# Gated linear attention behind its levels: state additions ahead, score products ahead of state products, two heads in turn, heads staggered

## Chip, cores and metric

The kernel runs on one core of one Trainium2 chip. The metric is the device time of one execution in microseconds (us); less is better. The time before is 3137.09 us, the median of three runs.

## What is computed

Two transformer blocks of two layers each. The change lies in the first layer of the second block, in its gated linear attention (GLA): 4 heads, keys of 64, values of 128, over 256 context tokens and 512 latent tokens, once forwards and once backwards in time. Cut to what matters:

```python
def gla_scan(q, k, v, loga, s0):              # chunk by chunk; loga: log of the decay of each key channel
    def step(S, inp):
        b = jnp.cumsum(ac, axis=2)
        ...
        attn = jnp.einsum('bhid,bhjd,bhijd->bhij', qc, kc, decay)
        o = attn @ vc + jnp.einsum('bhid,bhde->bhie', qc * jnp.exp(b), S)
        b_last = b[:, :, -1:, :]
        S_new = (jnp.exp(b_last[:, :, 0, :, None]) * S
                 + jnp.einsum('bhjd,bhje->bhde', kc * jnp.exp(b_last - b), vc))
...
    o_f, s_f = gla_scan(q, k, v, loga[0], s_f)
    o_b, s_b = gla_scan(flip(q), flip(k), flip(v), flip(loga[1]), s_b)
    o = o_f + flip(o_b)
    o = o * lax.rsqrt(jnp.mean(o * o, axis=-1, keepdims=True) + EPS)
    o = o.transpose(0, 2, 1, 3).reshape(B_, L, GLA_VAL_WIDTH) * g_gla.astype(jnp.float32)
    o = (o * jax.nn.silu(r.astype(jnp.float32))).astype(h.dtype)
    y = jnp.concatenate([fourier_mix(u_f), o], axis=-1) @ w_out
```

Each head's output is divided by its root mean square, scaled, multiplied by a gate and goes with the Fourier half into the output product `w_out`.

## The kernel before

Every engine has its own program in a fixed order, and semaphores join them: `k.tick(name, key)` counts up behind an instruction, `k.seen(name, key)` is what another engine (or the same) waits for. Nothing is reordered by a scheduler, so an instruction that waits holds up all that stands behind it on its engine. The data lie with features on partitions and tokens along the free dimension. There are 6 chunks of 128 tokens (`NC2`), and `f` counts two pairs of heads: heads 0 and 1 share one pair tile (head 0 on partitions 0 to 63, head 1 on 64 to 127), heads 2 and 3 the other.

The GLA stage has these parts.

- **Levels.** The scores with their decay are built in 14 steps (7 levels, forwards and backwards). In each, VectorE (DVE) makes an argument (L621, L622), ScalarE (ACT) takes its exponential (L628), DVE multiplies keys and queries in (L637), TensorE (PE) multiplies (L721), and DVE merges the result under a mask into `gatt` (L747). PE takes the heads there by turns, one on partitions 0 to 63, the next on 64 to 127 (`GL_UNITS`). The change doesn't touch the levels.
- **Decayed keys.** Behind the last merge DVE makes the argument for the forward keys (L2007), ACT the exponential (L1940), DVE the product with the keys (L2010). PE turns the result round by 12 transposes (L1892), ACT copies them out of PSUM (L1946), and the same `gcomb` is then used for the backward keys (L1948, L2010, L1892, L1946). Behind that come the decayed queries `e0` and `e1` (`gb` in the rows: L1949, L2012, L2013, L1951, L2015).
- **States.** For each of 5 steps and both directions PE makes the addition to the state, 4 matmuls (L1904, one per head, alternately into partitions 0 to 63 and 64 to 127 of PSUM), and DVE makes state = decay * state + addition (L2025, two instructions). In step n, PE waits for the backward state n. GpSimd (POOL) zeroes the first states (L1812) behind `e1`. The states lie over the queries and keys, in `z`.
- **Heads.** For each head and chunk PE adds up three products in PSUM: values with scores (L1918, contracted over 128 partitions), forward state with `e0` (L1919, over 64) and backward state with `e1` (L1920, over 64). Behind its 6 chunks the head is finished: ACT copies it out (L1957) and squares it (L1963), PE sums the squares over the partitions (L1924), ACT takes the root by Ln and Exp (L1968, L1971), DVE scales and gates (L2031, L2033), ACT and DVE split it into a high and a low part (L501, L507) for the output product. PE's next head follows its sum.
- **Output product.** `pe_out2` (L302 in the rows) waits for the low part of the last head.

The lines that order all this on PE and ACT:

```python
    for n in range(NC2 - 1):
        for d in range(2):
            ...
            if n:
                pe.wait_ge(*k.seen("state", ("g", 1, n)))
...
    for h in range(4):
        ...
        if h >= 2:
            pe.wait_ge(*k.seen("h_lo", ("gla", 4 + h - 2)))
...
            pe.wait_ge(*k.seen("squared", ("g", h, i)))
```

## Time and profile before

| | us |
|---|---|
| runs (three) | 3133.9, 3137.09, 3142.81 |
| median | 3137.09 |
| the profiled execution | 3133.24 |
| its span | 3131.9 |
| PE busy | 2682.8 (86%) |
| DVE busy | 1763.4 (56%) |
| ACT busy | 1063.2 (34%) |
| PE's share of the chain that ended last | 77% |
| the stage of the change, from the last merge to the output product | 1653.55 to 1748.59 |

The span runs from the first to the last instruction; the execution's own time has 1.3 us more around it. "Busy" is the time in which an engine ran instructions, and an engine that is busy need not be what the end waits for: that is told by the chain, followed back from the last instruction. PEclk is the clock that TensorE was granted, 1.0 for 2.4 GHz and 0.5 for 1.2 GHz. An fp32 matmul shows as two instructions, so "x48" on such a line are 24 matmuls; a transpose is one.

### The profile page before, as it was taken

The numbers are of one execution on the slowest core, as the hardware profiler recorded it, in microseconds if no ns is written. First come the engines' busy times: TensorE is split into PE (matmuls) and PEld (weight loads), VectorE is DVE, ScalarE is ACT, GpSimd is POOL, SyncE is SP. The second block draws the span as 40 slices with busy tenths as digits, with TensorE's granted clock in tenths as the row PEclk, the third lists the DMA queues.
The fourth block names the chain that finished last, engine by engine and source line by source line (L and its number), as shares of the span: only waits on it lengthen the run. The fifth ranks groups of instructions, "written<-read, shape, count | busy, mean of one in ns | idle before, by whom it ended". The sixth has DMA issues, their size and how long they took to land.

```text
span 3131.9 us, 31365 instructions
## 1 busy us (share of the span) xinstructions
PE 2682.8 (86%) x12792; PEld 2169.5 (69%) x12792; DVE 1763.4 (56%) x2386; ACT 1063.2 (34%) x1371; POOL 33.9 (1%) x52
## 2 busy tenths in 40 slices
PE   5956579999569999897676889999998866889998
PEld 4845458888448888685365778888886633578886
DVE  6574568888778877510483255424534155365464
ACT  3242253233343244422232253313324422254242
POOL 0000000000100000000200000000000000000000
PEclk9966789999779999999756899999998999999999
DMA  8700028855125666121000111211221100123232
GB/s 309 231 18 2 33 79 267 270 185 183 38 77 188 200 198 199 48 67 64 14 1 1 41 51 64 74 55 61 67 69 58 51 1 0 42 85 102 89 106 83
DMA packets 80270, 294.99 MB, mean 94 GB/s; under 512 B 8944, under 2 KB 11632, under 8 KB 79872
## 3 DMA queue, kind: packets, MB, share of 16 engines
q1 hardware_dynamic: 80128, 292.99, 28.6%
q8 instruction: 101, 1.65, 0.2%
q14 instruction: 41, 0.34, 0.0%
HBM read 290.86 MB, written 2.10 MB: 94 GB/s over the span
## 4 chain that ended last, share of the span: by engine, by line
PE 77%; DVE 13%; ACT 6%; issue 2%; DMA 0%; POOL 0%; SPq 0%; DVEq 0%; ACTq 0%
PE ps L302 65%; PE ps L721 2%; PE ps L2116 2%; PE ps L325 2%; PE ps L1744 1%; DVE anm L2243 1%; ACT h_hi L501 1%; DVE gatt L747 1%; ACT ascores L2195 1%; DVE h_lo L507 1%; ACT sq L1596 1%; DVE w_lo L283 1%; DVE aprobs L2218 1%; DVE x L1320 0%; DVE x L1333 0%
## 5 line engine op out<-in xcount | busy, mean ns | idle before, releaser
L302 PE MATMUL ps<-h_hi,w_hi 128*128 128x512 f32 (+1 forms) x2464 | 819.0, 369 | 68.5 <-DVE w_lo L283 38.4
L302 PE MATMUL ps<-h_hi,w_lo 128*128 128x512 f32 (+1 forms) x2464 | 815.8, 368 | 0.0
L302 PE MATMUL ps<-h_lo,w_hi 128*128 128x512 f32 (+1 forms) x2464 | 814.7, 367 | 0.0
L283 DVE TENSOR_TENSOR w_lo<-w_raw,w_hi 128x1024 fp32r<-128x1024 f32 (+2 forms) x323 | 414.7, 1284 | 617.4 <-ACT w_hi L275 616.6
L275 ACT ACTIVATE w_hi<-w_raw 128x1024 fp32r<-128x1024 f32 (+2 forms) x323 | 357.4, 1107 | 940.0 <-PE ps L302 917.5
L302 PEld LDWEIGHTS ps<-h_hi,w_hi 128*128 128x128 f32 x2464 | 466.1, 189 | 155.1 <-DVE w_lo L283 41.9
L302 PEld LDWEIGHTS ps<-h_lo,w_hi 128*128 128x128 f32 x2464 | 466.4, 189 | 77.4 <-issue 0.7
L302 PEld LDWEIGHTS ps<-h_hi,w_lo 128*128 128x128 f32 x2464 | 465.9, 189 | 77.6
L302 PE MATMUL ps<-g_hi,w_hi 128*128 128x512 f32 (+1 forms) x880 | 295.7, 369 | 0.8 <-DVE w_lo L283 0.8
L302 PE MATMUL ps<-g_lo,w_hi 128*128 128x512 f32 (+1 forms) x880 | 294.9, 368 | 0.0
L302 PE MATMUL ps<-g_hi,w_lo 128*128 128x512 f32 (+1 forms) x880 | 294.8, 368 | 0.0
L421 DVE CUSTOM_DVE_ANT_0 m_raw<-m_raw,c_act,small 128x1024 f32<-128x1024 f32 x179 | 226.4, 1280 | 2.8 <-DMA m_raw<-in_ada_w 2.8
L346 DVE SCALAR_TENSOR_TENSOR x<-ps,mods,x 128x512 f32<-128x512 f32 (+1 forms) x112 | 75.3, 690 | 211.7 <-PE ps L302 211.6
L302 PEld LDWEIGHTS ps<-g_hi,w_hi 128*128 128x128 f32 x880 | 165.3, 188 | 29.5 <-DVE w_lo L283 1.4
L302 PEld LDWEIGHTS ps<-g_lo,w_hi 128*128 128x128 f32 x880 | 165.3, 188 | 28.3 <-issue 0.5
L302 PEld LDWEIGHTS ps<-g_hi,w_lo 128*128 128x128 f32 x880 | 165.3, 188 | 27.8
L1463 DVE SCALAR_TENSOR_TENSOR conv_u<-ps,small,conv_u 128x510 f32<-128x510 f32 (+2 forms) x220 | 148.6, 692 | 3.1
L1419 ACT ACTIVATE g_hi<-gated 128x512 fp32r<-128x512 f32 (+1 forms) x88 | 60.4, 686 | 223.8 <-DVE gated L1476 223.8
L1414 ACT ACTIVATE silu_u<-conv_u 128x512 f32<-128x512 f32 (+1 forms) x88 | 60.4, 686 | 191.8 <-DVE conv_u L1463 191.8
L325 PE MATMUL ps<-h_hi,w_hi 128*128 128x512 f32 (+1 forms) x144 | 58.5, 444 | 73.1 <-DVE h_lo L507 38.5
L1478 DVE TENSOR_TENSOR g_lo<-gated,g_hi 128x512 fp32r<-128x512 f32 (+1 forms) x88 | 66.8, 759 | 66.2 <-ACT g_hi L1419 66.2
L325 PEld LDWEIGHTS ps<-h_hi,w_hi 128*128 128x128 f32 x144 | 30.5, 218 | 96.0 <-issue 73.2
(356 smaller groups left out, 2639.1 us busy)
## 6 DMA issues: line engine op xcount, KB each, us to landing
w_raw<-in_up SPq DMA_DIRECT2D x176, 512.0 KB, 3.5
m_raw<-in_w_mod SPq DMA_DIRECT2D x96, 512.0 KB, 3.5
w_raw<-in_down SPq DMA_DIRECT2D x64, 704.0 KB, 4.2
m_raw<-in_ada_w SPq DMA_DIRECT2D x83, 512.0 KB, 4.7
w_raw<-in_in SPq DMA_DIRECT2D x39, 512.0 KB, 3.5
w_raw<-in_out SPq DMA_DIRECT2D x16, 512.0 KB, 3.5
m_start<-in_ada_w SPq DMA_DIRECT2D x13, 512.0 KB, 11.7
w_raw<-in_qkv SPq DMA_DIRECT2D x12, 512.0 KB, 3.4
```

Of the source, the lines that this page charges most:

```text
L275: act.activation(k.w_hi[s][:, 0:w], k.w_raw[s][:, 0:w], ACT.Copy).then_inc(*k.tick("w_hi", g))
L283: dve.tensor_tensor(k.w_lo[s][:, 0:w], k.w_raw[s][:, 0:w], k.w_hi[s][:, 0:w].bitcast(F32), ALU.subtract).then_inc(*k.tick("w_lo", g))
L302: last = pe.matmul(ps[:, bank, 0:tn], a[:, c, :], b[:, c, t0:t0 + tn], start=c == 0 and n == 0, stop=c == kt - 1 and n == 2)
L325: last = pe.matmul(ps[:, bank, 0:tn], a, b[:, c, t0:t0 + tn], start=c == 0 and n == 0, stop=c == KD - 1 and n == 2)
L346: last = dve.scalar_tensor_tensor(x, k.ps[:, 2 * s + bank, 0:tn], gates[bank], x, ALU.mult, ALU.add)
L421: dve.tensor_tensor_reduce(w, w, k.c_act[:, last, :], 1.0, bias, ALU.mult, ALU.add, column(last)).then_inc(*k.tick("mods", job.key))
L721: last = pe.matmul(out, lhs[rows, cols], right, start=True, stop=True)
L1414: act.activation(f["silu"][:, :], f["conv"][0][:, :], ACT.Silu).then_inc(*k.tick("silu", g))
L1419: act.activation(f["hi"][:, j, :], f["g"][:, :], ACT.Copy).then_inc(*k.tick("g_hi", (block, layer, half, j)))
L1463: last = dve.scalar_tensor_tensor(o, ps[:, bank, lo - d:hi - d], w, o, ALU.mult, ALU.add)
L1478: dve.tensor_tensor(f["lo"][:, j, :], f["g"][:, :], f["hi"][:, j, :].bitcast(F32), ALU.subtract).then_inc(*k.tick("g_lo", key))
L2116: last = pe.matmul(k.ps[:, 6 + sl, :], k.av[:, j, (h // 4) * P:(h // 4 + 1) * P], k.aprobs[:, j, :], start=j == 0, stop=j == NS - 1)
```

## The change

The levels stay. Behind them:

- **Decayed keys.** The backward keys come first. They have their own buffer, which is free two steps before the levels end, so that ACT takes their exponential during the last levels; the forward keys have another (`gl_decayed_keys`). The transposes go through PSUM in three groups of four, banks 6 and 7, where it was a group of eight and one of four; ACT copies each group out by an instruction of its own. The exponential of the chunk ends has its own tile (`gexp`) and is taken early.
- **States.** PE makes the additions of one direction together (`pe_gl_add`): four of them without a wait, into two banks, the fifth behind state 2. DVE makes the states of one direction one behind the other, first backwards, then forwards. The first state is a copy of the addition, so POOL's zeroes go; the products with a zero state are left out (40 matmuls over 64 partitions where it was 48).
- **Heads.** Heads 0 and 1 are made together, then 2 and 3: first the products with the scores (`pe_gl_values`), then all products with states (`pe_gl_states`), the two heads by turns. PSUM holds all four heads, in banks 0 to 5. ACT copies a head with one instruction of 768 columns, squares it with one. The tail of a head (sum, root, scale, gate, split) is staggered against the next ones' (`pe_gl_sum`, `act_gl_root`).

The diff, cut: the removed lines are those of the functions printed above and are not shown again, but for POOL's.

```diff
         self.gends = gl("gends", [P, 2, 12])
+        self.gexp = gl("gexp", [P, 2, 12])
         an = Place(nc, at)
...
-    pool.wait_ge(*k.seen("q_decayed", "g"))
-    for d in range(2):
-        for f in range(2):
-            last = pool.memset(state[:, d, f * NC2 + GL_ORDER[d][0], :], 0.0)
-    last.then_inc(*k.tick("state_zero"))
...
     dve.wait_ge(*k.seen("gl_b", d))
+    if d == 0:
+        dve.tensor_copy(k.gends[:, 0, :].unsqueeze(2), e.rearrange("p (n c) -> p n c", c=CHUNK)[:, :, CHUNK - 1:CHUNK]
+                        ).then_inc(*k.tick("gl_ends"))
     if d == 1:
...
...
             pe.wait_ge(*k.seen("gl_biased", 1))
+    pe_gl_keys(k, 1)
+    pe_gl_values(k, 0, range(NC2))
+    pe_gl_add(k, 1)
+    pe_gl_keys(k, 0)
+    pe_gl_add(k, 0)
+    pe_gl_states(k, 0)
+    pe_gl_values(k, 2, range(2, NC2))
+    pe_gl_sum(k, 0)
+    pe_gl_values(k, 2, range(2))
+    pe_gl_states(k, 2)
+    for h in range(1, 4):
+        pe_gl_sum(k, h)
+def gl_decayed_keys(k, d):
+    return gl_combs(k)[1] if d == 0 else gl_combs(k)[2]
+def pe_gl_keys(k, d):
+    pe = k.nc.tensor
+    pe.wait_ge(*k.seen("kd", ("g", d)))
+    for b in range(3):
+        if d == 0 and b < 2:
+            pe.wait_ge(*k.seen("turned_out", ("gkd", 1, 2)))
+        elif b == 2:
+            pe.wait_ge(*k.seen("turned_out", ("gkd", d, 0)))
+        else:
+            pe.wait_ge(*k.seen("att", ("g", len(GL_STEPS) - 1, len(score_groups(GL_STEPS, len(GL_STEPS) - 1, 24)) - 1)))
+        for u, cols in enumerate(GL_FULL[4 * b:4 * b + 4]):
+            last = pe.matmul(k.ps[:, 6 + b % 2, u * P:(u + 1) * P], gl_decayed_keys(k, d)[:, cols], k.ident[:, :],
+                             is_transpose=True, start=True, stop=True)
+        last.then_inc(*k.tick("turn", ("gkd", d, b)))
+def gl_add_place(d, n):
+    return (6, 7, 2, 5)[2 * d + n // 2 % 2], n % 2
+def pe_gl_add(k, d):
+    pe = k.nc.tensor
+    pe.wait_ge(*k.seen("turned_out", ("gkd", d, 2)))
+    if d:
+        pe.wait_ge(*k.seen("att", ("g", len(GL_STEPS), len(score_groups(GL_STEPS, len(GL_STEPS), 24)) - 1)))
     for n in range(NC2 - 1):
+        c, (bank, half) = GL_ORDER[d][n], gl_add_place(d, n)
+        if n == 4:
+            pe.wait_ge(*k.seen("state", ("g", d, 2)))
+        for h in range(4):
+            rows = slice((h % 2) * 64, (h % 2) * 64 + 64)
+            last = pe.matmul(k.ps[rows, bank, half * 256 + (h // 2) * P:half * 256 + (h // 2 + 1) * P], k.gkdt[d][:, (h // 2) * NC2 + c, rows],
+                             k.v2[:, c, h * P:(h + 1) * P], start=True, stop=True)
+        last.then_inc(*k.tick("state_add", ("g", d, n)))
+def gl_mixed_at(h, c):
+    return (h % 2) * 3 * BANK + (h // 2) * TALL + c * CHUNK
+def gl_mixed(k, h):
+    return k.ps[:, 0:6, :].rearrange("p b c -> p (b c)")[:, gl_mixed_at(h, 0):gl_mixed_at(h, NC2)]
+def pe_gl_values(k, h0, chunks):
+    pe = k.nc.tensor
+    if h0 == 0:
+        pe.wait_ge(*k.seen("att", ("g", len(GL_STEPS), len(score_groups(GL_STEPS, len(GL_STEPS), 24)) - 1)))
+    elif 0 in chunks:
+        pe.wait_ge(*k.seen("mixed_out", ("g", 1)))
+    for h in (h0, h0 + 1):
+        for c in chunks:
+            pe.matmul(gl_mixed(k, h)[:, c * P:(c + 1) * P], k.v2[:, c, h * P:(h + 1) * P], k.gatt[:, GL_PLACE[h, c], :],
+                      start=c == 0 or gl_mixed_at(h, c) % BANK == 0, stop=False)
+def pe_gl_states(k, h0):
+    pe, (e0, e1), state = k.nc.tensor, gl_views(k)[2], gl_views(k)[6]
+    if h0 == 0:
+        pe.wait_ge(*k.seen("q_decayed", "g"))
+        pe.wait_ge(*k.seen("state", ("g", 0, NC2 - 1)))
+    f = h0 // 2
+    adds = [(h, c, d) for c in range(NC2) for d in range(2) if GL_ORDER[d][0] != c for h in (h0, h0 + 1)]
+    ends = {gl_mixed_at(h, c) // BANK: (h, c, d) for h, c, d in adds}
+    for h, c, d in adds:
+        rows = slice((h % 2) * 64, (h % 2) * 64 + 64)
+        last = pe.matmul(gl_mixed(k, h)[:, c * P:(c + 1) * P], state[rows, d, f * NC2 + c, :],
+                         (e0, e1)[d][rows, f * TALL + c * CHUNK:f * TALL + (c + 1) * CHUNK], start=False, stop=(h, c, d) in ends.values())
+    last.then_inc(*k.tick("mixed", ("g", h0)))
+def pe_gl_sum(k, h):
+    pe = k.nc.tensor
+    pe.wait_ge(*k.seen("squared", ("g", h)))
+    if h:
+        pe.wait_ge(*k.seen("root_log", ("g", h - 1)))
+    for t0, tn, bank in segments(TALL):
+        last = pe.matmul(k.ps[:, 6 + bank, 0:tn], k.ones[:, :], gl_squares(k, h)[:, t0:t0 + tn], start=True, stop=True)
+    last.then_inc(*k.tick("summed", ("g", h)))
+def gl_head(k, h):
+    return gl_combs(k)[2 if h < 2 else 0][:, (h % 2) * TALL:(h % 2 + 1) * TALL]
+def gl_squares(k, h):
+    return k.gkdt[0][:, :, :].rearrange("p n c -> p (n c)")[:, (h % 2) * TALL:(h % 2 + 1) * TALL]
 def act_gla(k):
...
     act_tables(k)
+    act.wait_ge(*k.seen("gl_ends"))
+    act.activation(k.gexp[:, :, :], k.gends[:, :, :], ACT.Exp, scale=s16).then_inc(*k.tick("end_decay", "g"))
+    act.wait_ge(*k.seen("scored", ("g", len(GL_STEPS) - 2, len(score_groups(GL_STEPS, len(GL_STEPS) - 2, 24)) - 1)))
+    act.activation(gl_decayed_keys(k, 1), e1, ACT.Exp, scale=s16).then_inc(*k.tick("kd_decay", ("g", 1)))
     act.wait_ge(*k.seen("kd_arg", "g"))
+    act.activation(gl_decayed_keys(k, 0), gl_decayed_keys(k, 0), ACT.Exp, scale=s16).then_inc(*k.tick("kd_decay", ("g", 0)))
+    act_gl_turned(k, 1)
     act.activation(e0, e0, ACT.Exp, scale=s16).then_inc(*k.tick("q_decay", ("g", 0)))
...
     act.activation(e1, e1, ACT.Exp, scale=s16).then_inc(*k.tick("q_decay", ("g", 1)))
+    act_gl_turned(k, 0)
     for h in range(4):
+        act.wait_ge(*k.seen("mixed", ("g", h // 2 * 2)))
+        act.activation(gl_head(k, h), gl_mixed(k, h), ACT.Copy).then_inc(*k.tick("mixed_out", ("g", h)))
         act.wait_ge(*k.seen("mixed_out", ("g", h)))
+        if h >= 2:
+            act.wait_ge(*k.seen("summed", ("g", h - 2)))
+        else:
+            act.wait_ge(*k.seen("state_add", ("g", 0, NC2 - 2)))
+        act.activation(gl_squares(k, h), gl_head(k, h), ACT.Square).then_inc(*k.tick("squared", ("g", h)))
         if h:
+            act_gl_root(k, h - 1)
+        if h >= 2:
+            act_high(k, "gla", 4 + h - 2, slice(0, TALL), gl_head(k, h - 2))
+    act_gl_root(k, 3)
+    for h in (2, 3):
+        act_high(k, "gla", 4 + h, slice(0, TALL), gl_head(k, h))
+def act_gl_turned(k, d):
+    act = k.nc.scalar
+    for b in range(3):
+        act.wait_ge(*k.seen("turn", ("gkd", d, b)))
+        got = k.ps[:, 6 + b % 2, :].rearrange("p (i t) -> p i t", t=P)
+        act.activation(k.gkdt[d][:, 4 * b:4 * b + 4, :], got, ACT.Copy).then_inc(*k.tick("turned_out", ("gkd", d, b)))
+def act_gl_root(k, h):
+    act = k.nc.scalar
+    act.wait_ge(*k.seen("summed", ("g", h)))
+    if h:
+        act.wait_ge(*k.seen("normed", ("g", h - 1)))
+    for t0, tn, bank in segments(TALL):
+        last = act.activation(k.rstd[:, t0:t0 + tn], k.ps[:, 6 + bank, 0:tn], ACT.Ln, scale=1.0 / P, bias=k.col("eps6"))
+    last.then_inc(*k.tick("root_log", ("g", h)))
+    act.wait_ge(*k.seen("root_log", ("g", h)))
+    act.activation(k.rstd[:, :], k.rstd[:, :], ACT.Exp, scale=-0.5).then_inc(*k.tick("root", ("g", h)))
 def dve_gla(k):
...
             dve_gl_gates(k, 1)
+    kd0, kd1 = (gl_decayed_keys(k, d) for d in range(2))
+    dve.wait_ge(*k.seen("kd_decay", ("g", 1)))
+    dve.tensor_tensor(kd1, kd1, kk, ALU.mult).then_inc(*k.tick("kd", ("g", 1)))
+    dve.wait_ge(*k.seen("scored", ("g", steps, len(score_groups(GL_STEPS, steps, 24)) - 1)))
+    dve.tensor_tensor(v3(kd0), wide(k.gends[:, 0, :]), v3(e0), ALU.subtract).then_inc(*k.tick("kd_arg", "g"))
+    dve.tensor_tensor(v3(e1), wide(k.gends[:, 1, :]), v3(e1), ALU.subtract).then_inc(*k.tick("q_arg"))
+    dve.wait_ge(*k.seen("kd_decay", ("g", 0)))
+    dve.tensor_tensor(kd0, kd0, kk, ALU.mult).then_inc(*k.tick("kd", ("g", 0)))
     dve.wait_ge(*k.seen("q_decay", ("g", 0)))
     dve.tensor_tensor(e0, e0, q, ALU.mult)
+    dve.wait_ge(*k.seen("kd", ("g", 0)))
+    dve.wait_ge(*k.seen("end_decay", "g"))
+    dve_gl_states(k, 1)
     dve.wait_ge(*k.seen("q_decay", ("g", 1)))
     dve.tensor_tensor(e1, e1, q, ALU.mult).then_inc(*k.tick("q_decayed", "g"))
+    dve.wait_ge(*k.seen("q_decayed", "g"))
+    dve_gl_states(k, 0)
     for h in range(4):
+        o = gl_head(k, h)
         dve.wait_ge(*k.seen("root", ("g", h)))
...
         dve.tensor_tensor(o, o, k.z2[:, 4 + h, :], ALU.mult).then_inc(*k.tick("value", ("gla", 4 + h)))
+        if h:
+            dve_low(k, "gla", 4 + h - 1, slice(0, TALL), gl_head(k, h - 1))
+    dve_low(k, "gla", 7, slice(0, TALL), gl_head(k, 3))
+def dve_gl_states(k, d):
+    dve, state = k.nc.vector, gl_views(k)[6]
+    for n in range(NC2 - 1):
+        c, nxt, (bank, half) = GL_ORDER[d][n], GL_ORDER[d][n + 1], gl_add_place(d, n)
+        dve.wait_ge(*k.seen("state_add", ("g", d, min(n | 1, NC2 - 2))))
+        if n:
+            dve.wait_ge(*k.seen("state", ("g", d, n)))
+        for f in range(2):
+            new, add = state[:, d, f * NC2 + nxt, :], k.ps[:, bank, half * 256 + f * P:half * 256 + (f + 1) * P]
+            if n:
+                at = f * NC2 + c
+                last = dve.scalar_tensor_tensor(new, state[:, d, at, :], k.gexp[:, d, at:at + 1], add, ALU.mult, ALU.add)
+            else:
+                last = dve.tensor_copy(new, add)
+        last.then_inc(*k.tick("state", ("g", d, n + 1)))
 def pe_out2(k):
```

How the order moves, at three places.

PE behind the levels. `gkdt_151` are the turned forward keys, `gkdt_152` the backward ones. Before, from the backward keys' transposes on:

```order
L1892 MATMUL ps<-ident,gcomb 128x128 [waits turned_out,kd]
L1892 MATMUL ps<-ident,gcomb 128x128 x7
L1892 MATMUL ps<-ident,gcomb 128x128 [waits turned_out]
L1892 MATMUL ps<-ident,gcomb 128x128 x3
L1904 MATMUL ps<-v_141,gkdt_151 64x128 [waits turned_out]
L1904 MATMUL ps<-v_141,gkdt_151 64x128 x3
L1904 MATMUL ps<-v_141,gkdt_152 64x128 x4
L1904 MATMUL ps<-v_141,gkdt_151 64x128 [waits state]
L1904 MATMUL ps<-v_141,gkdt_151 64x128 x3
L1904 MATMUL ps<-v_141,gkdt_152 64x128 [waits state]
L1904 MATMUL ps<-v_141,gkdt_152 64x128 x3
```

With the change, from the first transposes on:

```order
L1912 MATMUL ps<-ident,gcomb 128x128 [waits att,kd]
L1912 MATMUL ps<-ident,gcomb 128x128 x3
L1912 MATMUL ps<-ident,gcomb 128x128 [waits att]
L1912 MATMUL ps<-ident,gcomb 128x128 x3
L1912 MATMUL ps<-ident,gcomb 128x128 [waits turned_out]
L1912 MATMUL ps<-ident,gcomb 128x128 x3
L1957 MATMUL ps<-gatt,v_141 128x128 [waits att]
L1957 MATMUL ps<-gatt,v_141 128x128 x11
L1934 MATMUL ps<-v_141,gkdt_152 64x128 [waits att,turned_out]
L1934 MATMUL ps<-v_141,gkdt_152 64x128 x15
L1934 MATMUL ps<-v_141,gkdt_152 64x128 [waits state]
L1934 MATMUL ps<-v_141,gkdt_152 64x128 x3
```

The additions of a direction stand together, and 12 products with the scores (L1957, before L1918) stand between the backward keys' transposes and their additions.

PE at the heads. `z_142` are the states, `gb_147` and `gb_148` the decayed queries. Before, the end of head 0 and the start of head 1:

```order
L1918 MATMUL ps<-gatt,v_141 128x128
L1919 MATMUL ps<-gb_147,z_142 128x128
L1920 MATMUL ps<-gb_148,z_142 128x128
L1924 MATMUL ps<-tmp_67,ones 128x256 [waits squared]
L1924 MATMUL ps<-tmp_68,ones 128x512 [waits squared]
L1918 MATMUL ps<-gatt,v_141 128x128
L1919 MATMUL ps<-gb_147,z_142 128x128
```

With the change, the end of heads 0 and 1 and the start of heads 2 and 3:

```order
L1972 MATMUL ps<-gb_148,z_142 128x128 x2
L1972 MATMUL ps<-gb_147,z_142 128x128 x2
L1972 MATMUL ps<-gb_148,z_142 128x128 x2
L1957 MATMUL ps<-gatt,v_141 128x128 x8
L1983 MATMUL ps<-gkdt_151,ones 128x256 [waits squared]
L1983 MATMUL ps<-gkdt_151,ones 128x512
L1957 MATMUL ps<-gatt,v_141 128x128 [waits mixed_out]
L1957 MATMUL ps<-gatt,v_141 128x128 x3
L1972 MATMUL ps<-gb_148,z_142 128x128 x2
L1972 MATMUL ps<-gb_147,z_142 128x128 x4
```

The products over 128 partitions and those over 64 (L1972) no longer change places in each chunk, and 8 products of the next heads stand ahead of the first sum.

ACT at the heads. Before, head 1:

```order
L1957 ACTIVATE gcomb<-ps 128x256 [waits mixed]
L1957 ACTIVATE gcomb<-ps 128x512
L1963 ACTIVATE tmp_67<-gcomb 128x256 [waits summed,mixed_out]
L1963 ACTIVATE tmp_68<-gcomb 128x512 [waits summed]
L1968 ACTIVATE rstd<-ps,small 128x256 [waits normed,summed]
L1968 ACTIVATE rstd<-ps,small 128x512
L1971 ACTIVATE rstd<-rstd 128x768 [waits root_log]
L501 ACTIVATE h_hi<-gcomb 128x768 [waits value]
```

With the change, heads 0 and 1 and the start of head 2:

```order
L2020 ACTIVATE gcomb<-ps 128x768 [waits mixed]
L2026 ACTIVATE gkdt_151<-gcomb 128x768 [waits state_add,mixed_out]
L2020 ACTIVATE gcomb<-ps 128x768 [waits mixed]
L2026 ACTIVATE gkdt_151<-gcomb 128x768 [waits state_add,mixed_out]
L2050 ACTIVATE rstd<-ps,small 128x256 [waits summed]
L2050 ACTIVATE rstd<-ps,small 128x512
L2053 ACTIVATE rstd<-rstd 128x768 [waits root_log]
L2020 ACTIVATE gkdt_152<-ps 128x768 [waits mixed]
L2026 ACTIVATE gkdt_151<-gkdt_152 128x768 [waits summed,mixed_out]
L2050 ACTIVATE rstd<-ps,small 128x256 [waits normed,summed]
L2050 ACTIVATE rstd<-ps,small 128x512
```

Two heads are copied and squared before the first root, and the split of a head (L502, before L501) no longer stands right behind its root.

## Rows read from the trace of the kernel before

**Rows 1.** Two stretches: length; busy us of PE, PEld, DVE, ACT, POOL; PEclk; DMA.
```profile
1653.50:1690.20 36.70, 14.65 (x105) 12.03 (x105) 16.73 (x28) 8.84 (x9) 0.65 (x4) 0.59 0.00 1
1690.20:1748.60 58.40, 46.75 (x161) 32.68 (x161) 11.89 (x16) 19.13 (x33) 0.00 (x0) 0.62 0.00 0
```

**Rows 2.** Timeline of the decayed forward keys: start, us, engine, line, operation, [idle before <-releaser].
```profile
1653.74 1.76 DVE L2007 TENSOR_TENSOR gcomb<-gends,gb 128x1536 f32<-128x1536 f32 x1
1655.53 1.48 ACT L1940 ACTIVATE gcomb<-gcomb 128x1536 f32<-128x1536 f32 x1 [8.62 <-DVE gcomb L2007]
...
1658.86 2.82 PE L1892 MATMUL ps<-ident,gcomb 128*128 128x128 f32 x12 [6.55 <-DVE gcomb L2010]
1660.87 1.51 ACT L1946 ACTIVATE gkdt<-ps 128x1024 f32<-128x1024 f32 x2 [3.85 <-PE ps L1892]
```

**Rows 3.** Timeline of the state additions and the states, steps 0 and 1.
```profile
1669.17 1.10 PE L1904 MATMUL ps<-v,gkdt 128*64 128x128 f32 x16 [0.75 <-ACT gkdt L1946]
...
1677.31 0.65 POOL L1812 MEMSET z<- 128x128 f32 x4 [129.40 <-DVE gb L2015]
...
1679.37 1.98 PE L1904 MATMUL ps<-v,gkdt 128*64 128x128 f32 x16 [9.11 <-DVE z L2025]
1680.54 0.60 DVE L2025 SCALAR_TENSOR_TENSOR z<-z,gends,ps 128x128 f32<-128x128 f32 x2 [1.22 <-PE ps L1904]
```

**Rows 4.** Chain that ended last, one chunk of head 0, a piece of head 1.
```profile
1692.11 0.72 PE ps L1918 x2
1692.83 0.72 PE ps L1919 x2
1693.55 0.43 PE ps L1920 x2
...
1707.90 0.22 PE ps L1920 x2
```

**Rows 5.** Timeline of the last head's tail and the start of the output product.
```profile
1738.27 0.87 ACT L1957 ACTIVATE gcomb<-ps 128x256 f32<-128x256 f32 x2 [6.09 <-PE ps L1920]
...
1739.65 2.93 PE L1924 MATMUL ps<-tmp,ones 128*128 128x256 f32 x4 [1.41 <-ACT tmp L1963]
1742.61 1.05 ACT L1968 ACTIVATE rstd<-ps,small 128x256 f32<-128x256 f32 x2 [2.50 <-PE ps L1924]
1743.70 0.84 ACT L1971 ACTIVATE rstd<-rstd 128x768 f32<-128x768 f32 x1
1744.57 1.02 DVE L2031 SCALAR_TENSOR_TENSOR gcomb<-gcomb,small,rstd 128x768 f32<-128x768 f32 x1 [11.40 <-ACT rstd L1971]
...
1746.61 0.84 ACT L501 ACTIVATE h_hi<-gcomb 128x768 fp32r<-128x768 f32 x1 [2.08 <-DVE gcomb L2033]
...
1747.49 0.96 DVE L507 TENSOR_TENSOR h_lo<-gcomb,h_hi 128x768 fp32r<-128x768 f32 x1 [0.91 <-ACT h_hi L501]
```

**Rows 6.** Timeline of PE in the first levels, 64-partition products, heads by turns.
```profile
1551.78 1.16 PE L721 MATMUL ps<-z,gcomb 64*128 64x128 f32 x16 [2.62 <-DVE gatt L747]
1554.43 3.79 PE L721 MATMUL ps<-gkdt 64*128 64x128 f32 x32 [1.49 <-DVE gatt L747]
```

**Rows 7.** Timeline of the first block's linear attention, products over 128 partitions without a break.
```profile
264.94 5.14 PE L807 MATMUL ps<-v,z 128*128 128x128 f32 x24 [1.11 <-ACT z L852]
...
278.02 0.39 PE L816 MATMUL ps<-hatt,v 128*128 128x128 f32 x2
...
278.25 0.39 PE L817 MATMUL ps<-hk,z 128*128 128x128 f32 x2
...
282.04 3.60 PE L821 MATMUL ps<-z,ones 128*128 128x512 f32 x8
```

**Rows 8.** As rows 1: two stretches of the early levels, one of the output product.
```profile
1551.00:1553.00 2.00, 1.16 (x16) 0.97 (x16) 1.92 (x3) 0.00 (x0) 0.00 (x0) 1.00 0.00 0
1555.00:1557.00 2.00, 2.00 (x23) 2.00 (x22) 2.00 (x4) 0.98 (x1) 0.00 (x0) 0.50 0.00 0
1748.00:1754.00 6.00, 5.41 (x17) 4.66 (x18) 1.88 (x6) 0.40 (x1) 0.00 (x0) 0.50 0.24 87
```

89 lines of the change are left out of this document (removed).

## The prediction

> **What bounds the kernel now.** I read four views: the busy time and clock by stretches for the size of the stage, the timeline for its steps, the chain that ended last for what each waits on, and the timelines of other stages for shapes that are new here.
>
> The changed stage lasts 95 us of the span. In neither half is an engine full: up to the first head's products PE works 14.7 of 36.7 us, in the heads 46.8 of 58.4 us at a clock of 0.62 [rows 1]. It is a chain of handovers, so its length is the sum of steps that wait for each other, and the gain must be read from that chain, not from busy time. First the chain runs DVE, ACT, DVE, PE, ACT for the forward keys [rows 2] and once more through the same buffer for the backward ones; then each state step is 8 PE matmuls (1.98) and DVE behind them, which waits 1.22 us for the first four [rows 3]. In the heads it is PE all the way but for copy, square and sum: L1918 and L1919 take 0.72 us each at the low clock where L1920 takes 0.43; at the full clock L1920 takes 0.22 [rows 4]. All three stream 128 columns. The 0.29 us more falls on the matmul that changes between 128 and 64 contracted partitions; L1920, which stays on the same 64, pays nothing. Behind the last head, 10 us of tail stand alone [rows 5]. Everything outside the stage is the same instructions.
>
> **Prices.** At the low clock, all from rows: a transpose 0.235 us (2.82 / 12) [rows 2]; an addition matmul 0.25 (1.98 / 8), which shows that matmuls into alternating halves of the columns overlap, since one alone streams for 0.43 [rows 3, 4]; a 64-partition product with heads by turns 0.22 (16 in 3.79, with some 0.3 of run-out at the end) [rows 6], at 0.5 of the clock [rows 8]; a 128-partition product among its like 0.43 (5.14 / 12) [rows 7]; a sum 2.93 [rows 5]. At the full clock: addition 0.13, alternating product 0.12 [rows 3, 6, 8], 128-partition product 0.23 (278.02 to 278.25), sum about 1.5 (0.90 for 512 columns, 3.60 / 4) [rows 7]. ACT: 768 columns 0.84, 1536 columns 1.48 [rows 2, 5], so 0.83 ns a column and 0.2 fixed, and 0.6 for 512. Copy plus square of a head 1.75 with their handovers, Ln and Exp 1.95, scale and gate 2.05 [rows 5]. DVE on 1536 columns 1.76 [rows 2]; two state instructions 0.60 [rows 3]. A handover is 0.03 to 0.1.
>
> The Trainium skill, "ScalarE: Activation LUTs", section "Rules for kernel authors", budgets about 0.3 us per ACTIVATE plus 0.83 ns per element. By that a copy of 768 would take an estimated 0.94 and six copies of 512 would take 4.3; the trace's columns agree, its fixed part is smaller. The sum would be some 1 us longer by it.
>
> **The sum, part 1: to the first product with a state.** The new chain starts at 1653.6, ahead of where L2007 started [rows 2]. The exponential of the backward keys is made under the last levels, where ACT is idle, and costs nothing there; without that cover it would cost 1.5.
> - DVE multiplies the backward keys (1.8) and makes the forward argument (1.75), ACT takes the exponential (1.5): 1658.6. The first eight transposes (1.9) lie beside it. But the copies stand behind this exponential on ACT, so the third group of transposes comes late: copy 0.6, transposes 0.95: 1660.2.
> - PE is in order, so the 12 score products wait for that group, and they are not hidden: 12 x 0.43 = 5.15: 1665.4. Their gain is only the saved changes.
> - 16 additions 4.0, the fifth four 1.0 + 0.1: 1670.5. The backward states (5 x 0.63) run beside them, then `e1` (1.76), ending at 1673.
> - Forward keys: 12 transposes 2.8, last copy and handovers 0.75: 1674.0. The three copies per direction cost ACT 1.8 instead of 1.5, beside PE but for the last.
> - 20 additions 5.1, last state 0.75: 1679.9.
>
> The POOL zeroes (0.65 plus two handovers, 0.8) go from the path [rows 3]. The copy of the chunk ends moves into the first gates, where DVE is on the path too: 0.15 is only moved. Part 1 ends at 1679.9 instead of 1690.2, **10.2 us** earlier.
>
> **Part 2: the heads.**
> - 20 alternating products 4.4: 1684.4.
> - 8 score products of heads 2 and 3 with one change 3.65, beside copy and square of head 0 (1.75): 1688.0. Sum of head 0: 2.93: 1691.0.
> - 4 score products, a change, 20 alternating ones 6.3: 1697.3. Head 0's root, scale and gate (4.0) lie beside it. Sum of head 1: 1700.3.
> - ACT now is late next: root 1.95, high part of head 0 0.87, copy and square of head 3 1.75: 1704.9, then the root of head 2, whose Ln (1.05) frees PSUM: 1706.0. Sum of head 3: 1708.9.
> - Tail: root 1.95, scale and gate 2.05, high 0.85, low 1.0: 1714.8.
>
> The output product starts at 1714.8 instead of 1748.6: **33.7 us** less with the low clock everywhere. Against the span of 58.4 the heads give 23.5: 8 products with zero states, most of the changes (24 chunks x 2), the pairing, and three of four tails laid beside other heads.
>
> **The clock** is the unknown term. Before, the stage ran at 0.59 and 0.62 [rows 1], and at the full level in part of head 1, where L1920 took 0.22 [rows 4]. PE reached the full level in the first block's attention after a few us of 128-partition products without a break [rows 7]. The alternating products ran in one stretch at the full level, in the next at the low one [rows 8]. At the lower end nothing rises: 33.7. If it rises within the 12 score products, and from the first sum to the second, that gives 1.1 + 1.3 + 0.8 + 2.0 + 1.3, in all 40.2. I take **37 us**, the middle, since the stage before was at the full level about a quarter of the time. Against the profiled execution, 3133.2 - 37 = 3096; the median is 3.9 above that execution, so 3137.1 - 37 = **3100 us**.
>
> **Rivals.**
> 1. *Full clock throughout.* All PE terms fall to the second prices; the same chain gives 1696.9, 51.5 us less: 3086. For it: the denser PE. Against: every gap in parts 1 and 2, and idle stretches before at the low level. Chance 0.08.
> 2. *ACT bounds the heads.* Per head ACT has copy, square, Ln, Exp and high part, 4.4 us, 17.7 in all, and 3 us of DVE behind the last. From the end of the first state products (1684.4) nothing ends before 1705.2: a gain of 43 at most. It only trims rival 1 and is no case of its own. The rule is in the Trainium skill, "TensorEngine Tiling (Array Packing)", section "PSUM Bottleneck": tiling speeds TensorE up, not the emptying of PSUM, and it advises ScalarE and VectorE both; here ScalarE alone does it. By the forecast, sums and products still set the pace to 1697, so the rule is not yet met.
> 3. *The pairs don't overlap in an accumulation.* Rows 6 are products that don't add up in PSUM; these do. Then 0.43 each, 40 x 0.21 = 8.4 more: 25 us less, 3112. Worse, each change of head could cost what a change of contraction costs, 0.72: 40 x 0.5 = 20 more, 14 us less, 3123. Against: rows 6, same shape, same turns. The same page, section "Key Properties", says a change of tiling mode drains the engine and tiles of one mode work in parallel: that would be 0.22, as taken. Chance 0.07, a third of it for the worse form.
> 4. *Slower: the output product stays at the low clock.* It begins so before, too, at 0.50 [rows 8]: 17 instructions in 5.41 us, 0.64 per pair of 256 and 512 columns, and 0.32 more than at the full level. It has 192 pairs, 8 of them already slow. If the new tail, sparser at its end, kept the clock low for all others: 184 x 0.32 = 59 more, 3159. It turns the sign from 145 pairs on. Against: dense 128-partition work has always raised the clock before. Chance 0.02.
> 5. *Little changes*: an unforeseen wait on PE's order returns over 27 of the 37 us, such as the first transposes waiting for what the levels still hold. 3130. Chance 0.03.
>
> **How the numbers follow.** The forecast with its clock bounds has 0.80: 3097 to 3104, plus 3 to 4 us either way for the scatter of runs (3133.9 to 3142.8) and for the clock in the last levels, which is set by chance. The range reaches from rival 1 to rival 3's milder form: **3086 to 3113**. A measurement of this kernel tells 0.3%, 9.4 us, from no change. Faster by more: all but rivals 4 and 5, 0.95. Within: 0.03. Slower: 0.02.
>
> **What the new profile would show.** First transposes by 1655.5, score products from 1660 to 1665, five states of one direction 0.63 apart where they don't wait; 20 alternating products in 4.4 us, or 2.4 at the full level; the first of them at 1680; the forward additions from 1674; the output product at 1708 to 1716. I am wrong if the 20 alternating products take 8 us or more, if the score products are hidden, or if the difference in the whole doesn't lie between the last merge and the output product.

## The result and the profile after

| | before | after |
|---|---|---|
| median, us | 3137.02 (3133.9 to 3142.81) | 3084.35 (3081.81 to 3087.59) |
| ratio to before | 1 | 0.9831 [0.9813, 0.9848] |
| the profiled execution | 3133.24 | 3086.05 |
| its span | 3131.9 | 3084.7 |
| the stage, in that span | 95.0 | 46.5 |

The kernel is faster by 52.7 us where 37 were forecast. The time lies 1.65 us under the range. The same kernel measured again lies inside it (3090.51, below), so that it is outside by so little is chance; the 9.5 to 15.7 us between the two medians and the forecast of 3100 are not.

"The stage" runs from the start of DVE's first work behind the last merge to the output product's first row. Two stretches of it in the profile after, as in [rows 1], the first products with a state at 1677.1 between them, and the start of the output product:

```profile
1655.10:1677.10 22.00, 14.99 (x130) 13.13 (x130) 15.98 (x27) 7.48 (x9) 0.00 (x0) 0.74 0.00 1
1677.10:1701.50 24.40, 14.50 (x120) 10.28 (x120) 11.56 (x15) 17.75 (x25) 0.00 (x0) 0.84 0.00 1
1701.50:1707.50 6.00, 5.96 (x19) 5.13 (x20) 1.33 (x4) 0.00 (x0) 0.00 (x0) 0.51 0.28 87
```

PE works 29.5 us where it worked 61.4 [rows 1]. Its granted clock is 0.74 and 0.84 where it was 0.59 and 0.62. The last row shows that the output product still begins at the low level, as in [rows 8].

The timeline after, first half. It answers to [rows 2, 3]:

```profile
1655.09 1.74 DVE L2086 TENSOR_TENSOR gcomb<-gcomb,z 128x1536 f32<-128x1536 f32 x1
...
1656.88 1.97 PE L1912 MATMUL ps<-ident,gcomb 128*128 128x128 f32 x8 [3.03 <-DVE gcomb L2086]
...
1660.55 1.12 PE L1912 MATMUL ps<-ident,gcomb 128*128 128x128 f32 x4 [1.70 <-ACT gkdt L2041]
...
1661.46 5.22 PE L1957 MATMUL ps<-gatt,v 128*128 128x128 f32 x24
...
1666.61 1.97 PE L1934 MATMUL ps<-v,gkdt 128*64 128x128 f32 x32
...
1669.11 0.66 PE L1934 MATMUL ps<-v,gkdt 128*64 128x128 f32 x8 [0.53 <-DVE z L2123]
...
1669.70 1.09 PE L1912 MATMUL ps<-ident,spare 128*128 128x128 f32 x8
...
1672.39 1.97 PE L1934 MATMUL ps<-v,gkdt 128*64 128x128 f32 x32 [0.69 <-ACT gkdt L2041]
...
1674.19 2.73 DVE L2123 SCALAR_TENSOR_TENSOR z<-z,gexp,ps 128x128 f32<-128x128 f32 x8
...
1677.08 2.50 PE L1972 MATMUL ps<-gb,z 64*128 64x128 f32 x40 [1.56 <-DVE z L2123]
```

The 12 score products take 0.43 us each, the low level, and lie open on the path, as forecast. The 16 additions behind them take 1.97 us, 0.12 each: the clock has risen between the two, and it stays up to the last sum. In the last row 20 products by turns take 2.50 us, 0.125 each: the pairs overlap while they add up in PSUM.

The chain that ended last, from there to the output product. It answers to [rows 4, 5]:

```profile
1677.08 2.50 PE ps L1972 x40
1679.58 1.98 PE ps L1957 x16
1681.56 1.35 PE ps L1983 x4
1682.91 0.89 PE ps L1957 x8
1683.80 2.46 PE ps L1972 x40
...
1686.28 0.82 ACT gkdt L2020
...
1687.87 1.04 ACT rstd L2050 x2
...
1689.69 0.83 ACT h_hi L502
1690.51 0.71 ACT gkdt L2020
...
1691.99 1.04 ACT rstd L2050 x2
...
1693.17 2.36 PE ps L1983 x4
...
1701.41 0.14 issue
```

In these last 24.4 us PE is the chain for the first 9 us only. From 1686.3 on it is ACT, copy by copy and root by root, then one sum of PE and a tail as long as before. ACT works 17.75 of the 24.4 us.

The rest of the span didn't change by much: ahead of the stage the profile after is 1.5 us longer, behind its end 0.2 us shorter (3084.7 - 1701.55 against 3131.9 - 1748.59). Just ahead of the stage this can be seen in detail. The last 25.75 us of the levels are the same to the hundredth (before from 1627.80 to 1653.55, after from 1629.34 to 1655.09), with the exponential of the backward keys now made in them, so that costs nothing, as forecast. The stage begins anywhere between 1653.6 and 1663.1 in the profiles of this study (the kernel before at 1653.6 and 1658.6), since parts far ahead of it take a little more or less. So I compare stages, and whole times only beside them. Each stage length is that of one profile.

### The profile page after: what moved, and what is told of

Same layout as the page of the kernel before. It is cut to its first block, busy times and chain, and to the rows that moved or that the text cites. A ratio compares the mean times of both kernels' runs of the same rounds, so it can differ in the third digit from the quotient of the medians.

```text
span 3084.7 us, 31329 instructions
## 1 busy us (share of the span) xinstructions
PE 2653.8 (86%) x12776; PEld 2147.1 (70%) x12776; DVE 1762.1 (57%) x2386; ACT 1062.0 (34%) x1365; POOL 33.3 (1%) x48
## 3 DMA queue, kind: packets, MB, share of 16 engines
q8 instruction: 101, 1.65, 0.2%
## 4 chain that ended last, share of the span: by engine, by line
PE 77%; DVE 13%; ACT 6%; issue 2%; DMA 0%; POOL 0%; SPq 0%; DVEq 0%; ACTq 0%
PE ps L303 66%; PE ps L722 2%; PE ps L2208 2%; PE ps L326 2%; PE ps L1745 1%; DVE anm L2335 1%; ACT h_hi L502 1%; ACT ascores L2287 1%; DVE gatt L748 1%; DVE h_lo L508 1%; ACT sq L1597 1%; DVE w_lo L284 1%; DVE aprobs L2310 1%; DVE x L1321 0%; DVE x L1334 0%
```

## The experiments

**Theory A**, behind all of them: the order was costed rightly and only the clock wrongly. The new order brings PE to the full level by the first additions and keeps it there. **Theory B**: the clock is chance, or the gain came from elsewhere. Each expectation puts this into terms of its own run, so its letters are its own. Behind the two repeats, six runs change one part of the order each, and four put unread products into PE's gaps, two of them together with the first of the six changes. The clock within a stretch is read from the duration of the same instructions at either level.

### The same kernels again

> The changed kernel once more, unaltered, for the repeatability of its clock and its stage. If the level at which its parts run is set by the order of the work alone, its trace shows again: 12 score products at the low clock (5.2 us), 16 additions in 2.0, alternating products in 2.5 twice, last sum 1.5 to 2.9, output product slow for its first 5.5 us, and a stage of 45.5 to 47.5 us. If the clock is chance, the parts stand at other levels and the stage lies outside. Time 3080 to 3091.

> The kernel before once more, unaltered, for its stage: the first profile has 95.0 us from the first forward decayed keys to the output product's first row, with the low clock from the first state steps on. If the order sets the clock, the stage is 93 to 97 us again and the granted clock of the stretch of alternating products is 0.50. If the clock is chance, it may stand at full there, and the stage would be 75 to 85 us, and the gain of 48.6 us in the stage would be a gain of this pair of profiles alone.

The changed kernel: stage 44.5 us, 3090.51 us (3085.15 to 3095.05), ratio 0.9837 [0.9816, 0.9858]. Of its timeline on PE:

```profile
1669.31 3.80 PE L1957 MATMUL ps<-gatt,v 128*128 128x128 f32 x24
1673.03 1.97 PE L1934 MATMUL ps<-v,gkdt 128*64 128x128 f32 x32
...
1699.59 1.53 PE L1983 MATMUL ps<-gkdt,ones 128*128 128x256 f32 x4 [2.60 <-ACT rstd L2050]
```

The kernel before: stage 94.8 us (from 1658.6 to 1753.4), clock 0.50 from 1680 to 1700 and 0.64 from 1700 to 1750. In both profiles of it heads 1 and 2 ran mostly at the full level, heads 0 and 3 at the low one. So the stage's gain is 48.6 us in the first pair of profiles and 50.3 in the second. For each of these two kernels the level within the stage repeats, but for the edges. In the changed kernel the rise comes as the score products end or within them (5.22 or 3.80), and the last sum is at either level (2.35 or 1.53). These two make up the 2 us between the two profiles, and put the second 1 us under the lower bound of 45.5 that I had set for it.

### The score products behind the forward additions

```diff
-    pe_gl_values(k, 0, range(NC2))
     pe_gl_add(k, 1)
     pe_gl_keys(k, 0)
     pe_gl_add(k, 0)
+    pe_gl_values(k, 0, range(NC2))
```

> The changed kernel with the 12 score products of heads 0 and 1 behind the forward additions, right ahead of the products with states, where it had them behind the backward keys' transposes. In the changed kernel's trace they ran at the low clock (5.2 us for 12), the clock rose as they ended, and everything behind them up to the third sum ran at the full level. Theory A, these products without a break raise the clock: here the transposes, additions and states ahead of them run at the low level (an addition 0.25 us, not 0.13; granted clock 0.5 there), and the score products are at the low level again. From the last merge to the first product with a state it is 26 us instead of 22: 4 us slower. Theory B, the clock rises there anyway, by the time or by the additions: additions at 0.13, score products at 0.23 (2.8 us), and that stretch is 17 to 18 us: 4 us faster.

Stage 44.7 us; 3089.61 us (3085.24 to 3091.43), ratio 0.9825 [0.9796, 0.9854].

```profile
1670.02 3.68 PE L1934 MATMUL ps<-v,gkdt 128*64 128x128 f32 x32 [0.69 <-ACT gkdt L2041]
1674.31 0.66 PE L1934 MATMUL ps<-v,gkdt 128*64 128x128 f32 x8 [0.60 <-DVE z L2123]
...
1680.64 2.94 PE L1957 MATMUL ps<-gatt,v 128*128 128x128 f32 x24
1683.51 2.50 PE L1972 MATMUL ps<-gb,z 64*128 64x128 f32 x40
```

The first 16 additions take 3.68 us, so they start at the low level, and the fifth four already take 0.66. The score products aren't needed to raise the clock. Here they cost 2.9 us in place of 5.2, and the additions pay most of it back. From the start of the stage to the first product with a state it is 20.8 us, 22.0 in the first profile of the changed kernel: neither Theory A's 26 nor Theory B's 17 to 18. My idea that the score products are what brings the clock up fell. But the additions don't always do it either: in two later profiles of this order, those with unread products in the tail (below), the fifth four take 1.12 us and the 12 transposes behind them 2.92, both at the low level. What holds is that the forward additions are at the full level (1.97 us for 16) in every profile with the additions ahead, whichever work stands before them.

### Two heads in turn undone

```diff
-    adds = [(h, c, d) for c in range(NC2) for d in range(2) if GL_ORDER[d][0] != c for h in (h0, h0 + 1)]
+    adds = [(h, c, d) for h in (h0, h0 + 1) for c in range(NC2) for d in range(2) if GL_ORDER[d][0] != c]
```

> The changed kernel, but the products with states are made for one head after the other within each two, not by turns. Theory A, two heads on different partitions overlap: without the turns each of the 40 takes 0.22 us instead of 0.125 at the full clock, 2.5 us become 4.5 for each two heads: 3.5 to 4 us slower. Rival, the overlap gives nothing that the weight loads don't set anyway: same time within 0.5 us.

Stage 53.4 us; 3098.46 us (3090.89 to 3101.19), ratio 0.9848 [0.9811, 0.9884].

```profile
1682.62 6.58 PE L1972 MATMUL ps<-gb,z 64*128 64x128 f32 x40 [1.56 <-DVE z L2123]
1689.14 3.78 PE L1957 MATMUL ps<-gatt,v 128*128 128x128 f32 x16
1692.71 2.40 PE L1983 MATMUL ps<-gkdt,ones 128*128 128x256 f32 x4
...
1695.93 4.39 PE L1972 MATMUL ps<-gb,z 64*128 64x128 f32 x40
```

The last row is at the full level: 0.22 us a product one head after the other, against 0.125 by turns. That is 1.9 us for each pair of heads, 3.8 in all, what Theory A said. The rest is the clock, which it had left out: it fell in the first 20 products (6.58), which costs 2.2, and the 8 score products and the sum behind them pay another 1.7 and 0.9. In the second 20, in the same order, it stayed up. Undoing the turns costs 6.9 to 8.9 us of stage, against either profile of the changed kernel.

### The additions step by step

```diff
-        if n == 4:
-            pe.wait_ge(*k.seen("state", ("g", d, 2)))
+        if n:
+            pe.wait_ge(*k.seen("state", ("g", d, n)))
...
-        dve.wait_ge(*k.seen("state_add", ("g", d, min(n | 1, NC2 - 2))))
+        dve.wait_ge(*k.seen("state_add", ("g", d, n)))
```

> The changed kernel, but addition n of a direction waits for state n, and DVE takes each addition as it comes, so that the additions are no longer ahead. Theory A, the clock stays full over the short gaps: a step is 0.5 us of additions, 0.6 us of state and 0.2 of handovers; backward PE is 2.5 us later, forward states 1.9 us: 4.4 us slower. Rival, the gaps let the clock fall: additions at 0.25 and the products with states at 0.22, and the stage is 8 us or more slower.

Stage 54.0 us; 3093.46 us (3092.58 to 3098.13), ratio 0.9842 [0.9813, 0.9871].

```profile
1665.69 0.66 PE L1934 MATMUL ps<-v,gkdt 128*64 128x128 f32 x8 [0.69 <-DVE z L2125]
1667.06 0.66 PE L1934 MATMUL ps<-v,gkdt 128*64 128x128 f32 x8 [0.71 <-DVE z L2123]
1668.42 0.66 PE L1934 MATMUL ps<-v,gkdt 128*64 128x128 f32 x8 [0.71 <-DVE z L2123]
1669.79 1.12 PE L1934 MATMUL ps<-v,gkdt 128*64 128x128 f32 x8 [0.71 <-DVE z L2123]
1670.84 2.50 PE L1912 MATMUL ps<-ident,spare 128*128 128x128 f32 x12
...
1681.27 4.64 PE L1972 MATMUL ps<-gb,z 64*128 64x128 f32 x40 [0.79 <-DVE z L2123]
```

Each step is now PE, DVE, PE, 1.36 us apart, and PE idles over half of it. After four such steps the clock is down (1.12 where 0.66 stood), it is up again behind the transposes (the next four additions take 0.66), and after the forward steps it is down once more: the 20 products by turns take 4.64 us. That is my low-level forecast of 4.4 for them, measured. Making the additions ahead is worth 7.5 to 9.4 us, near the rival's 8 and not Theory A's 4.4. Of that, 3.4 lie between the first backward addition and the next transposes (6.5 us, 3.1 in the changed kernel), 2.5 between the first forward addition and the first product with a state (7.2 against 4.7), and 2.1 in the products by turns at the low level.

### Score and state products chunk by chunk

Two forms: head by head as in the kernel before, and with two heads in turn. Additions ahead and staggered tails stay in both.

```diff
-    pe_gl_values(k, 0, range(NC2))
...
-    pe_gl_values(k, 2, range(2, NC2))
...
-    pe_gl_values(k, 2, range(2))
...
-    adds = [(h, c, d) for c in range(NC2) for d in range(2) if GL_ORDER[d][0] != c for h in (h0, h0 + 1)]
+    adds = [(h, c, d) for h in (h0, h0 + 1) for c in range(NC2) for d in (-1, 0, 1) if d < 0 or GL_ORDER[d][0] != c]
...
+        if d < 0:
+            pe.matmul(gl_mixed(k, h)[:, c * P:(c + 1) * P], k.v2[:, c, h * P:(h + 1) * P], k.gatt[:, GL_PLACE[h, c], :],
+                      start=c == 0 or gl_mixed_at(h, c) % BANK == 0, stop=False)
+            continue
```

In the second form the list is `for c ... for d in (-1, 0, 1) ... for h in (h0, h0 + 1)`.

> The changed kernel, but the heads are made as before the change: head by head, chunk by chunk score product, forward state, backward state; no score products ahead. The placing in PSUM and the staggered tails stay. Theory A, the unbroken score products raised the clock: without them additions run at the low level and so do the heads, at 0.72 + 0.72 + 0.43 per chunk; 24 chunks take up to 40 us where 24 score and 40 state products took 13 in the changed kernel: 20 us or more slower. Theory B, the clock is full anyway: 0.42 + 0.42 + 0.22 per chunk, 24 us: 10 us slower.

> The changed kernel, heads 0 and 1 by turns, then 2 and 3, but per chunk: two score products, then the products with states; nothing of the scores ahead. So the turns stay and the unbroken run of score products goes; it is the fourth corner beside the changed kernel (from the last merge to the output product 46.5 us), heads one by one (53.4) and head by head and chunk by chunk (81.1). If the score products ahead and the turns are worth the same whatever the other does: 46.5 + (81.1 - 53.4) = 74. If what costs is the number of changes between 128 and 64 contracted partitions, 12 chunks x 2 instead of 24 x 2, and with them the clock: 57 to 64 us, and the granted clock in the heads tells how much of it is the clock: at the full level the chunks take 4 more us than the changed kernel, at the low level 12 to 18.

The first: stage 81.1 us; 3121.96 us (3116.06 to 3138.97), ratio 0.9944 [0.9923, 0.9964]. The second: stage 54.8 us; 3099.79 us (3094.59 to 3111.6), ratio 0.9887 [0.9864, 0.991]. A piece of PE's timeline in the first (L1971 are the score products, L1975 those with states):

```profile
1680.58 0.79 PE L1971 MATMUL ps<-gatt,v 128*128 128x128 f32 x2
1681.31 1.22 PE L1975 MATMUL ps<-gb,z 64*128 64x128 f32 x4
```

and in the second:

```profile
1676.51 0.71 PE L1971 MATMUL ps<-gatt,v 128*128 128x128 f32 x4
1677.15 0.71 PE L1975 MATMUL ps<-gb,z 64*128 64x128 f32 x8
```

Then a stretch of the head products in each, in the order of [rows 1]:

```profile
1697.00:1714.00 17.00, 17.00 (x53) 12.32 (x51) 1.98 (x2) 1.89 (x3) 0.00 (x0) 0.50 0.00 0
```

```profile
1688.00:1694.00 6.00, 6.00 (x56) 4.79 (x55) 1.97 (x2) 0.54 (x2) 0.00 (x0) 1.00 0.00 0
```

One head's chunk costs 1.88 us in the first (1680.58 to the next such row at 1682.46), with the clock at 0.50; a chunk of two heads costs 1.29 in the second (1676.51 to 1677.80), at 1.00. In both stretches PE has no gap. So the old order of the heads pays for the changes between 128 and 64 partitions and for products that don't overlap, and in this run also for the clock. It fell in the third chunk and stayed at 0.50 to the output product.

This order doesn't always run at the low level, though. In the kernel before, the same products head by head stood at the full level in head 1 and at the low one in head 3, both without a gap:

```profile
1708.00:1712.00 4.00, 4.00 (x25) 3.10 (x24) 2.74 (x3) 0.84 (x1) 0.00 (x0) 1.00 0.02 4
1732.00:1736.00 4.00, 4.00 (x15) 3.10 (x14) 0.96 (x1) 0.18 (x1) 0.00 (x0) 0.50 0.00 0
```

A chunk took 1.06 us in the first of these rows. No run here shows what decides between the two. As an estimate from these prices: 16 chunks with two states at 1.88 us and 8 with one at 1.44 would be 1.06 and 0.84 at the full level, so that of the 35 to 37 us that this run is longer than the changed kernel some 16 are the clock and the rest is changes and missing overlap.

Against the expectations: the 24 chunks of the first run take 39.8 us of PE's time, as Theory A said, but not for its reason, since the additions reached the full level without the score products (the fifth four took 0.66 us). The second run lies below both of its forecasts, 74 and 57 to 64 us; its chunks are at the full level, and it is 8.3 to 10.3 us longer than the changed kernel.

When the stretch begins in the first form the clock is still full and a product with its change takes 0.42 us (1674.50 to 1674.92 to 1675.34); by 1676.8 it takes 0.72, which is [rows 4]. A change of contraction therefore costs 0.29 us at the low level (0.72 - 0.43) and 0.20 at the full one (0.42 - 0.22). That there is a drain at such changes the Trainium skill states in "TensorEngine Tiling (Array Packing)", section "Key Properties"; the size comes from these rows.

### The tails in sequence

```diff
     pe_gl_sum(k, 0)
...
+    pe_gl_sum(k, 1)
     pe_gl_values(k, 2, range(2))
     pe_gl_states(k, 2)
-    for h in range(1, 4):
+    for h in range(2, 4):
...
-        if h:
-            act_gl_root(k, h - 1)
-        if h >= 2:
-            act_high(k, "gla", 4 + h - 2, slice(0, TALL), gl_head(k, h - 2))
-    act_gl_root(k, 3)
-    for h in (2, 3):
+        act_gl_root(k, h)
         act_high(k, "gla", 4 + h, slice(0, TALL), gl_head(k, h))
```

> The changed kernel, but each head's tail (copy, square, sum, root, scale and gate, high and low part) is finished before the next one's starts, as before the change. If three tails were hidden by the staggering: a tail is 0.84 + 0.84 + 1.5 + 1.9 + 2.0 + 0.84 = 7.9 us, four are 31.7 in a row instead of 22 from the first copy to the output product: 10 us slower, 56.5 us in the stage. Rival, ACT's 4.4 us per head set the pace anyway and the order gives little: under 3 us slower.

Stage 60.6 us, 14.2 to 16.1 longer; 3105.21 us (3104.22 to 3106.23), ratio 0.99 [0.9883, 0.9916]. Of ACT's timeline:

```profile
1697.58 1.05 ACT L2046 ACTIVATE rstd<-ps,small 128x256 f32<-128x256 f32 x2 [3.02 <-PE ps L1984]
1698.66 0.85 ACT L2049 ACTIVATE rstd<-rstd 128x768 f32<-128x768 f32 x1
1701.58 0.84 ACT L502 ACTIVATE h_hi<-gcomb 128x768 fp32r<-128x768 f32 x1 [2.08 <-DVE gcomb L2102]
1702.33 0.79 ACT L2021 ACTIVATE gkdt<-ps 128x768 f32<-128x768 f32 x1
```

For the four heads ACT waits 1.65, 3.02, 2.53 and 3.02 us for the sum, and each time 2.08 us for DVE's scale and gate, with the next head's copy queued behind. The forecast was 56.5 us. It took every sum at the full level; but PE now waits 6.52 us ahead of two of them and 3.03 ahead of one, and these three take 2.93, 2.44 and 2.93 us, 3 to 4 us more in all than in the changed kernel. With the heads made as fast as this, the stagger is the largest part of the change among those undone alone. The kernel before had the long products of the next head beside each tail but the last; here the products are too short for that.

### Unread products in PE's gaps

These test the clock alone: products of 512 columns whose result nobody reads, 1, 2 and 7 of them in the gaps of the tail.

```diff
-    for h in range(1, 4):
+    for h, n in ((1, 1), (2, 2), (3, 7)):
         pe_gl_sum(k, h)
+        pe_gl_warm(k, n)
+def pe_gl_warm(k, n):
+    for _ in range(n):
+        k.nc.tensor.matmul(k.ps[:, 3, 0:LAT], k.ones[:, :], k.z2[:, 4, 0:LAT], start=True, stop=True)
```

> The changed kernel with matmuls over 128 partitions that nothing reads, into a PSUM bank that is free: one (0.86 us) behind the sum of head 1, two behind that of head 2, seven behind that of head 3, where PE waited 1.3, 2.6 and 6.8 us. If only PE's idle time lets the clock fall: the last sum takes 1.5 instead of 2.4 us and the output product starts at the full level, so that its first products take 0.35 us per pair and not 0.64 over 5.6 us: 0.8 + 2.6 us faster. Rival, the clock falls all the same or PE is late for the output product: no gain.

> Both: score products of heads 0 and 1 behind the forward additions (44.7 us in its run, 1.7 less than the changed kernel's 46.5), and the unread matmuls in the tail. If the two add up: stage 43 to 44 us, and the output product's first 5.6 us at the full level, 2.6 less: about 5 us faster than the changed kernel. If the gain of the late score products was where the clock rose by chance: 46 in the stage.

> The order with the score products behind the forward additions, and the unread products in the tail, once more and in as many rounds as the unaltered kernel beside it. Theory A: its stage is 1.5 us shorter (as it was in the first run of that order, 44.7) and its output product 2.6 us shorter, so 2 to 4 us under the unaltered kernel. Theory B: the shorter stage was the chance of the clock (46.1 was seen with the warm tail), and only 2 to 3 us of the output product remain, near what the runs scatter.

The warm tail: stage 45.9 us, the last sum at 1.53 us; 3088.17 us (3082.25 to 3089.01), ratio 0.984 [0.9826, 0.9855]. With the late score products: stage 46.1 both times; 3088.11 us (3080.67 to 3090.49) and 3085.51 us (3082.43 to 3092.54). The output product's first row with the warm tail:

```profile
1706.69 0.59 PE L303 MATMUL ps<-h_hi,w_hi 128*128 128x256 f32 x2 [0.34 <-DVE h_lo L508]
```

In its first 20 us PE issues 116 matmul instructions of the output product, against 100 or 101 in both profiles of either unaltered kernel. At 0.174 each at the full level that is 2.8 us won, and in all four profiles with a warm tail it is there. In the whole time it can't be seen: the runs of one kernel lie mostly 6 to 10 us apart. The late order doesn't shorten the stage: 44.7 in its first profile, 46.1 in the next two. The 1.4 us between them are the fifth four additions and the transposes behind them, at the full level in the first profile and at the low one in the others. That is Theory B of the last of these expectations.

One more run fills the gaps ahead of the score products too. Here `pe_gl_warm` takes the bank as a third argument and reads `v2`; the products in the tail stay:

```diff
     pe = k.nc.tensor
+    if d:
+        pe.wait_ge(*k.seen("att", ("g", len(GL_STEPS) - 1, len(score_groups(GL_STEPS, len(GL_STEPS) - 1, 24)) - 1)))
+        pe_gl_warm(k, 3, 6)
     pe.wait_ge(*k.seen("kd", ("g", d)))
     for b in range(3):
+        if d and b == 2:
+            pe.wait_ge(*k.seen("att", ("g", len(GL_STEPS), len(score_groups(GL_STEPS, len(GL_STEPS), 24)) - 1)))
+            pe_gl_warm(k, 2)
```

> Unread matrix products (512 columns, into banks that nobody reads at the time) fill TensorE's gaps ahead of the first transposes (3), ahead of the third group of backward transposes (2), and in the tail (1, 2 and 7). Theory A, the clock is what is left of the miss: it then stands at full by the 12 score products, which take 2.6 us instead of 5.2, and the stage is 42.5 to 44 us with the output product at full from its first row; time 3 to 6 us under the unaltered kernel of this call. Theory B, the clock rises only in the score products as before, since what runs ahead of them is too short: stage 46 to 48 and only the tail's gain of about 3 us. Either way no part outside the stage moves.

Stage 43.15 us; 3084.63 us (3079.6 to 3098.4), ratio 0.9826 [0.9803, 0.9849].

```profile
1658.48 4.30 PE L1898 MATMUL ps<-v,ones 128*128 128x512 f32 x6
1662.61 1.04 PE L1924 MATMUL ps<-ident,gcomb 128*128 128x128 f32 x8
...
1665.74 2.84 PE L1969 MATMUL ps<-gatt,v 128*128 128x128 f32 x24
```

The clock is up at the first transposes (1.04 where 1.97 stood), and the score products take 2.84. This is the chain at the full level from the first transposes on, as Theory A said, 1.4 to 3.3 us shorter than the two unaltered profiles. Its median is 5.9 us under that of the unaltered kernel measured beside it, but its runs lie 19 us apart and the intervals overlap, so I don't call it faster.

## Why the prediction was wrong, step by step

The chain was right for the clock that it assumed, and one term was mis-sized: **the clock**. I wrote "I take 37 us, the middle, since the stage before was at the full level about a quarter of the time". Step by step, in us (the two profiles of the changed kernel):

| step | forecast, low level | after | again |
|---|---|---|---|
| start to the first score product | 6.6 | 6.4 | 6.4 |
| 12 score products | 5.15 | 5.15 | 3.7 |
| 20 backward additions | 5.1 | 3.1 | 3.1 |
| forward keys turned | 3.55 | 2.7 | 2.7 |
| 20 forward additions, last state | 5.85 | 4.7 | 4.7 |
| 20 products by turns | 4.5 | 2.4 | 2.4 |
| 8 score products, sum of head 0 | 6.6 | 3.2 | 3.2 |
| 4 score products, 20 by turns | 6.3 | 3.4 | 3.4 |
| to the end of head 3's sum | 11.6 | 9.4 | 8.5 |
| tail | 5.9 | 6.0 | 6.3 |
| sum | 61.2 | 46.5 | 44.5 |

- **Right**: the first step, the score products at the low level and open on the path, the tail. None of my three signs of being wrong showed. No step but the tail is longer than forecast, and where the clock was low (the products by turns at 4.64 in the run of steps, the sums at 2.93 in the tails in sequence) the low prices hold.
- **The clock term.** With the low level throughout I had 33.7 us of gain; as measured it is 48.6 and 50.3. My upper bound of 40.2 let the clock rise "within the 12 score products", which happened (at their end in the first profile), but then counted only single pieces of the rest. It was up for all of it, but for the last sum in the first profile. The rows that shrink most are the middle of the table, and together the rows lie 14.7 and 16.7 us under the low-level forecast. The reasoning that failed is taking the old order's share of time at the full level for the new order. That share said nothing on single pieces: the same products ran at the full level in heads 1 and 2 of the kernel before and at the low one in heads 0 and 3, and in the run chunk by chunk, head by head, they fell to 0.50 in the third chunk. The new order held the full level from the forward additions to the sum of head 2 in all seven profiles that keep its additions ahead, its grouping, its turns and its stagger. Why it holds it is not shown. What is shown is that its parts help: with the turns, the grouping, the additions ahead or the stagger undone, pieces of the stage fell to the low level.
- **Rival 1**, full clock throughout, chance 0.08, is nearly what came. Its chain ends 43.3 us behind the start; the run with the gaps filled has 43.15. The changed kernel is 1 to 3 us from it, in the first products and the last sum. Its gain is 51.7 us by its own end of 1696.9, not 51.5. Against it I had held "every gap in parts 1 and 2". In the changed kernel the gaps of 1.3 and 1.6 us did not bring the clock down; behind the one of 2.6 us ahead of the last sum it was down in the first profile and up in the second.
- **Rival 2**, ACT bounds the heads. I made it no case of its own, rightly for the low level. At the full level it is met: from the end of the first products by turns I had 20.8 us as the least, and it is 22.0. PE works 12.1 of them, ACT 17.75. It is 21.5 in the second profile, and filling the rest of PE's time with unread products leaves it at 21.5. So PE is mostly no longer what the heads wait for. The Trainium skill says that tiling speeds up TensorE but not the emptying of PSUM ("TensorEngine Tiling (Array Packing)", section "PSUM Bottleneck"). The trace agrees in part: ACT is the bound, but only its four copies and four Ln read PSUM, 7.4 of its 17.75 us.
- **Rival 3**, pairs that don't overlap, fell: 0.125 us a product by turns, 0.22 not by turns. Rival 4 fell in its strong form: the output product starts slow and is at the full level some 6 us on, as before. A slow pair costs 0.29 us more there (0.64 against 0.35), not 0.32. Rival 5 fell.
- **The forward additions**: DVE is late there, not PE. It needs 2.73 us for four states, and PE, done with all additions after 3.1 us, waits 1.56 us for the last state.
- **The whole.** The two stages' gains, 48.6 and 50.3, stand beside 52.7 and 49.4 in the medians. The differences are within what runs of one kernel scatter. In the first pair of profiles the spans differ by 47.2 us. Of that the stage gives 48.6, the part behind it 0.2, and the part ahead of it takes 1.5 back.

What each part is worth when it alone is undone: stagger 14 to 16 us, grouping by contraction (with turns kept) 8 to 10, additions ahead 7.5 to 9.4, turns 7 to 9. Grouping and turns undone together cost 35 to 37, far more than their sum. In that run, and in no other of these, the clock was low through nearly all of the heads, some 16 us by the estimate above. These worths hold for this chain with its clock, each with what its run did to the clock. They are read from one profile for each run against two of the changed kernel. What the early backward exponential and the missing zero states are worth was not run by itself.

## What to carry to other kernels

Where a stage is a chain on TensorE with a granted clock between the two levels, cost the new order twice, all low and all full, and ask which of the new pieces would bring it down; the share of time at the full level in the old order says little. Group matmuls by their contraction, take disjoint tiles by turns, and then look at once at who empties PSUM: after the change the stagger of ScalarE's work was worth more than either. Small gains in such a stage must be read from the stage in the trace, since the whole time scatters by more.

## What the runs showed of the hardware

- PE without a gap ran at either level. With products of 128 and 64 partitions head by head it was busy 17.00 of 17.00 us at 0.50 in the run chunk by chunk, and in the kernel before 4.00 of 4.00 us at 1.00 in head 1 and at 0.50 in head 3. With the same products for two heads in turn it was 6.00 of 6.00 at 1.00. In the last levels PE was busy 10.00 of 10.00 us at 0.50 (1650 to 1660 in the repeat of the changed kernel).
- Five profiles have the backward additions, in alternating column halves, right behind the transposes. In all five the first 16 take 3.68 us. In three the next four are at the full level (0.66), in two at the low one (1.12).
- Products by turns cost 0.125 us each at the full level and 0.23 at the low one (4.64 / 20), within an accumulation as outside it [rows 6].
- Steps of 0.66 us of work and 0.7 of idle brought the clock down after four of them. Single gaps went either way. In the changed kernel gaps of 1.3 and 1.6 us did not bring it down. In the kernel before, the sums of heads 1 and 2 took 2.93 us, the low level, behind a wait of 1.41 us, though the heads had run at the full level, and so in both profiles. With two heads in turn chunk by chunk a sum took 2.93 us behind a wait of 1.78.
